# Inputs rearranged before launch, transposed activations, and a seven-slot weight ring in a float32 two-layer model kernel

## The chip, the cores and the metric

The kernel runs on one core of a Trainium2 chip. The metric is device time in microseconds (us), the median of several runs. The core has five engines with queues of their own: TensorE (PE in the rows, matrix products), VectorE (DVE), ScalarE (ACT), GpSimd (POOL) and SyncE (SP, which here only issues transfers), and sixteen DMA engines that move data between HBM and the on-chip memory. An engine works through its own queue in order and waits on semaphores for the others.

## The reference, cut to what matters

The program is a mixing layer followed by two attention-like layers, all in float32, on 256 tokens of width 2048. Only its start matters for the change:

```python
shift, scale, gate = split(silu(c) @ w_ada + b_ada, 3)            # w_ada is 2048 x 6144
shift_c, scale_c, _ = split(silu(c_ctx) @ w_ada + b_ada, 3)
hc = rmsnorm(ctx, g_pre) * (1 + scale_c) + shift_c                 # 256 context tokens
zc = hc @ w_in[:, :XBC_W + DT_W]
hx = rmsnorm(x, g_pre) * (1 + scale) + shift                       # 256 tokens
zx = hx @ w_in                                                     # w_in is 2048 x 12352
...
vn = rmsnorm(v, g_v)
sg = einsum('gqk,bckgd->bcqgd', w_s, vn) + b_s                     # 16 matrices of 128 x 128
...
x = x + gate * rmsnorm(mixed @ w_out, g_post)
```

Here rmsnorm divides a token's row by the root of its mean square. The products are made from float32 numbers split in a high and a low part (`w_hi`, `w_lo`, `h_hi`, `h_lo`), three passes for each product.

## The kernel before, in words

Every engine has its own block of code, and the order of its work is written out by hand; semaphores tie the engines together. Weights stream through four slots of 512 columns by 2 row blocks (`raw`), ScalarE makes the high part (`w_hi`), VectorE the low part (`w_lo`), and TensorE multiplies. A set of eight such units over the 2048 rows is a chunk.

The first part of the program, the prefix, does more at once. For both token sets `x` and `ctx` it needs the normalised rows transposed (`x_T`, features on the partitions), and for every feature the scale and shift from `w_ada` (`mod`). The prefix is a list, `PREFIX`, that TensorE walks through:

- `turn` (16 entries, L741): four 128x128 transposes of the normalised rows in `x_in` each; ScalarE and VectorE take turns in copying the results to `x_T`.
- `ada` (32 entries, eight groups e of four, L718): one 1 MB block of `w_ada` times the two vectors `silu(c)` and `silu(c_ctx)` in `c_wide`, four matrix products. The rows print two instructions for each of these products, so x8 is one block and x32 a whole group.
- `cols` (L726): after four blocks VectorE copies the sums out (`ada_rows`), TensorE transposes them, and VectorE makes two feature blocks of `mod` (L1943 to L1951). ScalarE then computes `h_f` and `h_hi` from `x_T` and `mod` (`modulate`, L1290) and VectorE the low part `h_lo` (`halve`, L2025).
- `w` (16 entries, L623): one unit of the first two chunks, 24 products for an even m, 16 for an odd m. Unit m needs `h` of the feature blocks of group m // 2.

From group 3 on the list repeats: four `ada`, unit 2e-3, `cols` e, unit 2e-2. After group 7 come units 13, 14 and 15, and then the chunk B1.

SyncE walks through `LOADS`: the same order, with each unit's load placed four entries ahead. A block of `w_ada` is two DMAs of 512 KB with rows of 1 KB (256 columns), and is put in one of six slots (three in `raw_early`, three in `raw_first`); from the seventh block on SyncE waits until TensorE has used the slot. `x` and `ctx` are loaded as rows (8 KB each) ahead of all this. GpSimd issues twelve small loads of vectors (bias, gains, convolution weights) as rows, which TensorE transposes (`turn_vec`, L706), and later, when TensorE has used 28 blocks, the rest of the constants.

Before the transposes, ScalarE squares the rows of `x_in` and sums them in the same instruction (L1270, four of 128x2048), VectorE makes means and reciprocals, and both scale the rows (L2018, L1279).

Later, in phase V, the sixteen matrices of `w_s` come as rows and are turned by TensorE in four hooks (`turn_ws`, L861) and copied by VectorE (`w_sT`, L2175). In phases S and O1 the gate third of `w_ada` comes in 32 blocks (`gate_w`).

Of the kernel before, what the change touches and what calls it, by code (L numbers as in the profile page):

```python
# [11 lines left out]
P = 128  # L12
# [45 lines left out]
VEC_ROWS = [sum(k for _, k in rows) for rows in VEC_TILES]  # L58
# [52 lines left out]
PREFIX = []  # L111
for _v in range(AW4):
    PREFIX += [("turn", 0, 4 * _v + x) for x in range(4)] + [("ada", 0, _v)]
# [85 lines left out]
def two_blocks_kernel(nc, ins, out):  # L199
# [34 lines left out]
    RAW6 = at("raw_first", 136, [P, 6, 4, 2, 256])  # L234
    RAW3 = at("raw_early", 48, [P, 3, 4, 2, 256])
    ada_raw = lambda n: (RAW3 if n < 3 else RAW6)[:, ada_slot(n)]
# [10 lines left out]
    IDR = at("ident_r", kb, [P, P], F32R); kb += 0.5  # L247
# [11 lines left out]
    XIN = at("x_in", 128, [P, 2, NT, D])  # L259
    XT = at("x_T", 80, [P, 2, KT, SEQ])  # L260
    JUNK = at("junk", 112, [P, D])
# [4 lines left out]
    VR = at("vec_rows", 184, [P, 4, P])  # L266
# [18 lines left out]
    WS = at("w_s_rows", 160, [P, MLP_G, P])  # L285
    WST = at("w_sT", 176, [P, MLP_G, P])
# [76 lines left out]
    with ctx:  # L363
        def sem(name):
# [10 lines left out]
        vec_turned, vec_ok, ada_done, ada_ok, mod_ok = sem("vec_turned"), sem("vec_ok"), sem("ada_done"), sem("ada_ok"), sem("mod_ok")  # L375
        xn_ok, rec_ok, xa_ok = sem("xn_ok"), sem("rec_ok"), sem("xa_ok")
        pair_ok, zero_ok = sem("ident_pair_ok"), sem("zero_ok")
        turned, h_ok = sem("turned"), sem("h_ok")
# [5 lines left out]
        ws_in, gv_in, ctx_in = sem("ws_in"), sem("gv_in"), sem("ctx_in")  # L384
        ws_turned, ws_ok, v_ok, vstd_ok, vn_ok, sg_done, sg_ok = (sem(n) for n in (
            "ws_turned", "ws_ok", "v_ok", "vstd_ok", "vn_ok", "sg_done", "sg_ok"))
# [37 lines left out]
        class Seq:  # L424
# [24 lines left out]
            "w_out_odd_2": dram["w_out_odd_2"][0], "w_ada": dram["w_ada"][0],  # L449
        }  # L450
        w_of = {n: w.rearrange("(t p) n -> p t n", p=P) for n, w in w_of.items()}

        def vec_load(eng, tiles, t0, names, signal):

            for t, rows in enumerate(tiles, t0):
                for n, k in rows:
                    if names is not None and (n in ("c", "c_ctx")) != (names == "c"):
                        continue
                    if n.startswith("conv_w"):
                        src = dram["conv_w"][0].rearrange("k (b p) -> (k b) p", p=P)  # L460
                        src = src[0:128] if n == "conv_w0" else src[128:160]
                    else:
                        a = dram[n]
                        while len(a.shape) > 1 and a.shape[0] == 1:
                            a = a[0]
                        src = a if len(a.shape) == 2 else a.rearrange("(r p) -> r p", p=P)
                    r0 = VEC[n][1]
                    eng.dma_start(VR[r0:r0 + k, t, :], src).then_inc(signal, 16)
# [133 lines left out]
        def _(pe):  # L602
# [126 lines left out]
            def turn(x):  # L729

                a, k0 = x // 8, x % 8 * 2
                if x == 0:
                    pe.wait_ge(xn_ok, 2)
# [2128 lines left out]
```

## Time and profile before

| what | value |
|---|---|
| median of 3 runs | 1957.72 us (1957.55 to 1961.33) |
| span of the profiled execution | 1955.8 us, first to last instruction |
| outside the span, median less span | 1.9 us |
| TensorE busy | 1909.1 us, 98% |
| VectorE, ScalarE, GpSimd busy | 62%, 51%, 5% |
| moved by DMA | 360.49 MB, mean 184 GB/s |
| mean granted TensorE clock | 0.993 |

The profiled execution has no time of its own beside its span, so the 1.9 us between the span and the median stand for what lies around it. Busy shares are of the span. A matrix product's printed duration runs past the start of the next, because they are pipelined: what counts in a stretch is the distance from one start to the next. The 40 slices of the page show a TensorE that is below 90% busy in the first slice only (each slice is 48.9 us), and DMA engines that are full in the first two and a half slices and half full later.

### The profile page before, as it was taken

What the parts mean: (1) busy time and instruction counts of PE and PEld (TensorE: products, weight loads), DVE (VectorE), ACT (ScalarE), POOL (GpSimd) and SP (SyncE); (2) the same over time, 40 slices, a digit from 0 to 9 for tenths busy, and PEclk for the clock granted to TensorE, in tenths of its full rate; (3) what the DMA queues carried; (4) which work ended last, traced back from release to release, by engine and by line L of the source; (5) the groups of instructions that cost most, each with busy time, mean ns of one, the idle gap of its engine ahead of it and who ended that gap; (6) DMA issues with size and microseconds to landing.
All of it is one profiled execution on the core that took longest, in us unless ns stands there. A gap on an engine that the chain in (4) does not pass through costs nothing.

```text
span 1955.8 us, 28973 instructions
## 1 busy us (share of the span) xinstructions
PE 1909.1 (98%) x11133; PEld 1608.1 (82%) x11133; DVE 1217.1 (62%) x1703; ACT 1000.0 (51%) x1464; POOL 106.6 (5%) x117
## 2 busy tenths in 40 slices
PE   5989999999999999999999999999999999999999
PEld 3558888898887777787888998878889999998887
DVE  3325655686558889867766687667555455555554
ACT  5435322345555666654446434667444555556642
POOL 1010000000023344000000000000000000000000
PEclk8989999999999999999999999999999999999999
DMA  9983322357657667758975555545566655555564
GB/s 341 349 255 108 100 85 86 87 171 226 191 175 196 183 174 202 234 175 264 357 249 153 151 152 162 171 142 152 181 186 176 181 171 162 173 164 170 167 188 163
DMA packets 210046, 360.49 MB, mean 184 GB/s; under 512 B 14264, under 2 KB 61776, under 8 KB 209024
## 3 DMA queue, kind: packets, MB, share of 16 engines
q1 hardware_dynamic: 200448, 349.36, 57.9%
q10 hardware_dynamic: 8848, 8.47, 2.1%
q8 instruction: 86, 1.41, 0.3%
q0 software_dynamic: 624, 0.92, 0.2%
q14 instruction: 40, 0.33, 0.1%
HBM read 356.55 MB, written 2.16 MB: 183 GB/s over the span
## 4 chain that ended last, share of the span: by engine, by line
PE 89%; DVE 3%; SPq 2%; DMA 1%; ACT 1%; issue 1%; DVEq 0%; ACTq 0%
PE acc L656 53%; PE acc L643 15%; PE acc L623 10%; DMA raw_first<-in_w_ada 1%; SPq L502 1%; PE side L902 1%; PE side L1029 1%; DVE conv L2088 1%; PE side L956 1%; PE side L891 1%; DVE w_lo L1921 1%; PE side L796 1%; PE side L623 0%; ACT w_hi L1241 0%; PE side L718 0%
## 5 line engine op out<-in xcount | busy, mean ns | idle before, releaser
L1921 DVE TENSOR_TENSOR w_lo<-raw,w_hi 128x1024 fp32r<-128x1024 f32 (+1 forms) x552 | 670.7, 1220 | 418.5 <-ACT w_hi L1241 412.5
L1241 ACT CAST w_hi<-raw 128x1024 fp32r<-128x1024 f32 (+1 forms) x544 | 561.0, 1035 | 607.9 <-PE acc L656 398.0
L656 PE MATMUL acc<-w_hi,h_hi 128*128 128x512 f32 (+1 forms) x1312 | 521.3, 397 | 2.5 <-DVE h_lo L2286 1.8
L656 PE MATMUL acc<-w_hi,h_lo 128*128 128x512 f32 (+1 forms) x1312 | 509.0, 388 | 0.0
L656 PE MATMUL acc<-w_lo,h_hi 128*128 128x512 f32 (+1 forms) x1312 | 508.3, 387 | 0.0
L656 PEld LDWEIGHTS acc<-w_hi,h_hi 128*128 128x128 f32 x1312 | 246.7, 188 | 52.8 <-DVE h_lo L2286 2.1
L656 PEld LDWEIGHTS acc<-w_hi,h_lo 128*128 128x128 f32 x1312 | 246.4, 188 | 51.1
L656 PEld LDWEIGHTS acc<-w_lo,h_hi 128*128 128x128 f32 x1312 | 246.9, 188 | 47.0
L643 PE MATMUL acc<-h_hi,w_hi 128*128 128x256 f32 x896 | 257.8, 288 | 1.0 <-DVE h_lo L2286 1.0
L643 PE MATMUL acc<-h_hi,w_lo 128*128 128x256 f32 x896 | 254.5, 284 | 0.0
L643 PE MATMUL acc<-h_lo,w_hi 128*128 128x256 f32 x896 | 254.5, 284 | 0.0
L643 PEld LDWEIGHTS acc<-h_hi,w_hi 128*128 128x128 f32 x896 | 172.9, 193 | 2.0 <-DVE h_lo L2286 1.4
L643 PEld LDWEIGHTS acc<-h_lo,w_hi 128*128 128x128 f32 x896 | 173.0, 193 | 0.2
L643 PEld LDWEIGHTS acc<-h_hi,w_lo 128*128 128x128 f32 x896 | 172.8, 193 | 0.0
L623 PE MATMUL acc<-h_hi,w_hi 128*128 128x512 f32 x352 | 141.4, 402 | 4.2 <-DVE w_lo L1921 3.0
L623 PE MATMUL acc<-h_hi,w_lo 128*128 128x512 f32 x352 | 138.4, 393 | 0.0
L623 PE MATMUL acc<-h_lo,w_hi 128*128 128x512 f32 x352 | 138.4, 393 | 0.0
L656 PE MATMUL acc<-w_hi,g_hi 128*128 128x512 f32 x256 | 101.0, 395 | 0.0
L656 PE MATMUL acc<-w_hi,g_lo 128*128 128x512 f32 x256 | 99.9, 390 | 0.0
L656 PE MATMUL acc<-w_lo,g_hi 128*128 128x512 f32 x256 | 99.7, 390 | 0.0
L623 PEld LDWEIGHTS acc<-h_hi,w_hi 128*128 128x128 f32 x352 | 66.8, 190 | 20.8 <-issue 3.8
L623 PEld LDWEIGHTS acc<-h_hi,w_lo 128*128 128x128 f32 x352 | 66.8, 190 | 14.5
(405 smaller groups left out, 1977.5 us busy)
## 6 DMA issues: line engine op xcount, KB each, us to landing
raw<-in_w_in SPq DMA_DIRECT2D x184, 512.0 KB, 4.2
raw<-in_w_in_odd SPq DMA_DIRECT2D x128, 512.0 KB, 3.7
raw<-in_w_in_even SPq DMA_DIRECT2D x96, 512.0 KB, 3.8
raw<-in_w_out SPq DMA_DIRECT2D x64, 512.0 KB, 5.0
raw_first<-in_w_ada SPq DMA_DIRECT2D x58, 512.0 KB, 8.8
gate_w<-in_w_ada SPq DMA_DIRECT2D x32, 512.0 KB, 6.4
raw<-in_w_out_even SPq DMA_DIRECT2D x32, 512.0 KB, 4.6
raw<-in_w_out_odd SPq DMA_DIRECT2D x32, 512.0 KB, 4.6
```

Of the source, the lines that this page charges most:

```text
L502: sp.dma_start(ada_raw(n)[:, :, h, :], w_of["w_ada"][:, 4 * u:4 * u + 4, h * D + e * 256:h * D + e * 256 + 256]).then_inc(ada_in[ada_slot( ...
L623: o = nc.tensor.matmul(bank[b][:].rearrange("p (a t) -> p a t", a=2), l, r, start=first and kk == 0 and x == 0, stop=last and kk == 1 and ...
L643: o = nc.tensor.matmul(ACC[b][:, (b4 % 2) * SEQ:(b4 % 2 + 1) * SEQ], l, r, start=first and kk == 0 and m == 0 and b4 % 2 == 0, stop=last a ...
L656: o = nc.tensor.matmul(ACC[b][:, 0:n], l, r, start=first and kk == 0 and m == 0, stop=last and kk == 1 and m == 2)
L796: o = nc.tensor.matmul(SB[d][:, g * 256:(g + 1) * 256], BG[:, t, g, :], XW[:, d, t, g * 256:(g + 1) * 256], start=t == 0, stop=t == NT - 1)
L891: o = nc.tensor.matmul(SB[3 - 2 * d][:, t * 256:(t + 1) * 256], GB[:, 1, t * P:(t + 1) * P], ST[:, d, bass.ds(g * 256, 256)], start=True, ...
L902: o = nc.tensor.matmul(SB[2][c:c + 64, t * 256 + r * HD:t * 256 + (r + 1) * HD], MM[:, r % 2, k, t * P + c:t * P + c + 64], XH[:, k, bass. ...
L956: o = nc.tensor.transpose(SB[b][:, k * SEQ + t * P:k * SEQ + (t + 1) * P], src[:, t, kt * P:(kt + 1) * P], con("ident"))
L1029: o = nc.tensor.matmul(later(SB[2 * (n % 2)][c:c + 64, o0:o0 + 64], l), KI[:, hb, h, k * P + c:k * P + c + 64], right(QD[:, hb, h, sl], l) ...
L1241: act.copy(WHI[:, u % 4, :, 0:n], RAW[:, u % 4, :, 0:n]).then_inc(hi_ready, 1)
L1921: dve.tensor_tensor(WLO[:, u % 4, :, 0:n], RAW[:, u % 4, :, 0:n], WHI[:, u % 4, :, 0:n].bitcast(F32), ALU.subtract).then_inc(lo_ready, 1)
L2088: seq(dve.scalar_tensor_tensor(v[:, 0:end], z[:, k:k + end], w(k), v[:, 0:end], ALU.mult, ALU.add))
```

## The change

The arrays are rearranged before the launch, outside the device time, and the kernel loads them in the form in which it uses them.

- `x` and `ctx` come transposed in four blocks of 1 MB (`x_cols`), straight into `x_T`. The 64 transposes, their copies and the scaling of rows go. The sums of squares are now over the transposed data: ScalarE squares 128x2048 blocks (`x_squares`), VectorE adds eight feature blocks per token (`x_reduce`, a reduction whose successive elements lie 1 KB apart), TensorE sums over the partitions with a vector of ones (`x_sums`) and spreads the reciprocal roots over all partitions (`x_rows`), ScalarE copies them (`x_rstd_rows`), and VectorE multiplies `x_T` by them, one feature block (128x512) at a time (`x_scale`): eight ahead of group 0, the other eight in pairs behind the groups 1 to 4.
- The small vectors come as columns in three DMAs; their transposes go.
- `w_ada` comes in contiguous blocks of 1 MB, 8 KB for each partition, one DMA each; the first weight units come in blocks with 4 KB or 2.5 KB for each partition. Ten blocks of `w_ada` fit before SyncE waits (three early slots used once, and a ring of seven).
- `w_s` comes transposed, so the sixteen transposes and four copies go. The gate blocks come contiguous, 4 KB for each partition.
- The low part of unit 0 is now made ahead of `halve` 0 and 1.

```diff
-PREFIX = []
-for _v in range(AW4):
-    PREFIX += [("turn", 0, 4 * _v + x) for x in range(4)] + [("ada", 0, _v)]
+PREFIX = [("ada", 0, v) for v in range(AW4)]
...
-    LOADS.insert(_at - (4 if _m < 14 else 0), ("w", 0, _m))
-VEC_AT = 14
+    LOADS.insert(max(AW4, _at - (4 if _m < 14 else 0)), ("w", 0, _m))
+EARLY, RING = 3, 7
...
-    return n if n < 6 else 3 + n % 3 if n % 6 < 3 else n % 3
+    return n if n < EARLY else EARLY + (n - EARLY) % RING
...
         def _(sp):
             sp.dma_start(CON[:, 0:P], dram["const_a"][:, 0:P]).then_inc(con_in, 16)
-            sp.dma_start(XIN[:, 0], dram["x"][0].rearrange("(t p) d -> p t d", p=P)).then_inc(x_in, 16)
-            sp.dma_start(XIN[:, 1], dram["ctx"][0].rearrange("(t p) d -> p t d", p=P)).then_inc(ctx_in, 16)
+            for i in range(4):
+                sp.dma_start(XT[:, i // 2, i % 2 * 8:i % 2 * 8 + 8, :].rearrange("p k t -> p (k t)"), dram["x_cols"][i]).then_inc(xt_in[i], 16)
             for kind, e, u in LOADS:
                 if kind == "ada":
                     n = AW4 * e + u
-                    if n == 9:
-                        sp.wait_ge(turned, KT)
-                    elif 6 <= n < 9:
-                        sp.wait_ge(ada_used, n - 2)
-                    elif n >= 12:
-                        sp.wait_ge(ada_used, n - 5)
-                    for h in range(2):
-                        sp.dma_start(ada_raw(n)[:, :, h, :],
-                                     w_of["w_ada"][:, 4 * u:4 * u + 4, h * D + e * 256:h * D + e * 256 + 256]
-                                     ).then_inc(ada_in[ada_slot(n)], 16)
+                    if n >= EARLY + RING:
+                        sp.wait_ge(ada_used, n - RING + 1)
+                    sp.dma_start(ada_raw(n).rearrange("p j h n -> p (j h n)"), dram["ada_units"][n]).then_inc(ada_in[ada_slot(n)], 16)
...
-            sp.dma_start(WS[:], dram["w_s"][0].rearrange("g q k -> q g k")).then_inc(ws_in, 16)
+            sp.dma_start(WST[:].rearrange("p g q -> p (g q)"), dram["w_s_cols"]).then_inc(ws_in, 16)
...
+            def x_sums():
+
+                pe.wait_ge(sc_ok, 3)
+                for a in range(2):
+                    pe.wait_ge(xss_ok, 2 * a + 2)
+                    for t in range(NT):
+                        for i in range(2):
+                            o = nc.tensor.matmul(ACC[0][:, 2 * a + t:2 * a + t + 1], SSX[:, 2 * a + i, t * P:(t + 1) * P],
+                                                 STAT[:, 63:64], start=i == 0, stop=i == 1)
+                o.then_inc(xsum_done, 1)
+
+            def x_rows():
+
+                pe.wait_ge(nrt_ok, 3)
+                for x in range(4):
+                    o = nc.tensor.matmul(ACC[1][:, x * P:(x + 1) * P], STAT[:, 12 + x:13 + x].to_broadcast([P, P]), con("ident"),
+                                         start=True, stop=True)
+                o.then_inc(xrow_done, 1)
...
+            def x_squares(i):
+
+                act.wait_ge(xt_in[i], 16)
+                if i >= 2:
+                    act.wait_ge(xss_ok, i - 1)
+                act.activation(SQX[i % 2][:], XT[:, i // 2, i % 2 * 8:i % 2 * 8 + 8, :], ACT.Square).then_inc(nsq_ok, 1)
...
+            def x_reduce(i):
+
+                dve.wait_ge(nsq_ok, i + 1)
+                dve.tensor_reduce(SSX[:, i, :], SQX[i % 2][:].rearrange("p k t -> p t k"), AX.X, ALU.add).then_inc(xss_ok, 1)
...
+            def x_scale(kt):
+
+                if kt == 0:
+                    dve.wait_ge(xrow_ok, 1)
+                dve.tensor_tensor(XT[:, :, kt, :], XT[:, :, kt, :], RBX[:], ALU.mult).then_inc(xr_ok, 1)
...
-            chunk("V", cV + 1, 1, hooks={u: (lambda u=u: turn_ws(u)) for u in range(4)})
+            chunk("V", cV + 1, 1)
```

TensorE at the start of the program, before:

```order
L699 MATMUL side<-con,vec_rows 128x32
L741 MATMUL acc<-con,x_in 128x128 x16
L718 MATMUL side<-raw_early,c_wide 32x512 x4
L741 MATMUL acc<-con,x_in 128x128 x16
L718 MATMUL side<-raw_early,c_wide 32x512 x4
L741 MATMUL acc<-con,x_in 128x128 x16
L718 MATMUL side<-raw_early,c_wide 32x512 x4
```

TensorE at the same place in the changed kernel (`x_square_sums` is what VectorE's reductions wrote, `stat` holds the vector of ones and the reciprocal roots):

```order
L691 MATMUL acc<-stat,x_square_sums 128x1 x8
L699 MATMUL acc<-con,stat 128x128 x4
L673 MATMUL side<-raw_early,c_wide 32x512 x12
L673 MATMUL side<-raw_first,c_wide 32x512 x4
L681 MATMUL side<-con,ada_rows 128x128 x4
L673 MATMUL side<-raw_first,c_wide 32x512 x8
```

The transposes between the first blocks are gone, and all four blocks of group 0 now stand behind twelve small products that need the sums of squares of all of `x` and `ctx`.

VectorE at the start, before:

```order
L1927 TENSOR_TENSOR ident_pair<-con 128x64
L2011 TENSOR_SCALAR stat<-stat 128x2
L2016 RECIPROCAL stat<-stat 128x2
L2018 TENSOR_SCALAR x_in<-x_in,stat 128x2048 x2
L1958 COPY x_T<-acc 128x512 x2
L2011 TENSOR_SCALAR stat<-stat 128x2
L2016 RECIPROCAL stat<-stat 128x2
L2018 TENSOR_SCALAR x_in<-x_in,stat 128x2048
L1958 COPY x_T<-acc 128x512 x6
L1934 COPY ada_rows<-side 128x512
```

VectorE at the start of the changed kernel:

```order
L1848 TENSOR_TENSOR ident_pair<-con 128x64
L1879 TENSOR_REDUCE x_square_sums<-x_squares_a 128x256
L1879 TENSOR_REDUCE x_square_sums<-x_squares_b 128x256
L1879 TENSOR_REDUCE x_square_sums<-x_squares_a 128x256
L1879 TENSOR_REDUCE x_square_sums<-x_squares_b 128x256
L1884 TENSOR_SCALAR stat<-acc 128x4
L1886 RECIPROCAL stat<-stat 128x4
L1892 TENSOR_TENSOR x_T<-x_T,x_rstd_rows 128x2x256 x8
L1855 COPY ada_rows<-side 128x512
```

Four reductions and eight products now stand ahead of the copy of the first group's sums, in place of three scalings and eight copies.

SyncE from its first transfer, before:

```order
L489 DMA con<-in_const_a 128x128
L490 DMA x_in<-in_x 128x2x2048
L491 DMA x_in<-in_ctx 128x2x2048
L502 DMA raw_early<-in_w_ada 128x4x256 x4
L513 DMA raw<-in_w_in 128x2x512
L502 DMA raw_early<-in_w_ada 128x4x256 x2
L502 DMA raw_first<-in_w_ada 128x4x256 x2
```

SyncE from its first transfer in the changed kernel:

```order
L468 DMA con<-in_const_a 128x128
L470 DMA x_T<-in_x_cols 128x2048 x4
L476 DMA raw_early<-in_ada_units 128x2048 x3
L476 DMA raw_first<-in_ada_units 128x2048
L481 DMA raw<-in_w_even 128x1024
L481 DMA raw<-in_w_odd 128x2x320
L476 DMA raw_first<-in_ada_units 128x2048 x4
```

A block of `w_ada` is one transfer now, and the first weight unit's load has moved behind the four blocks of group 0.

## Rows read from the trace of the kernel before

**Rows 1.** The page's head and TensorE's line: busy, share, instructions.

```profile
span 1955.8 us, 28973 instructions
PE 1909.1 (98%) x11133; PEld 1608.1 (82%) x11133; DVE 1217.1 (62%) x1703; ACT 1000.0 (51%) x1464; POOL 106.6 (5%) x117
```

**Rows 2.** TensorE's waits after 170 us, longest first.

```profile
PE side L956 <- DVE x L2357: 3.2, 1, 3.2
```

**Rows 3.** Stretches of the prefix: busy time, granted clock, DMA share, GB/s.

```profile
core 0: us, PE busy (x) PEld busy (x) DVE busy (x) ACT busy (x) POOL busy (x), PEclk, DMA share, GB/s
4.00:14.00 10.00, 0.31 (x1) 0.18 (x1) 0.39 (x2) 5.93 (x9) 3.47 (x8) 1.00 1.01 403
20.00:120.00 100.00, 89.71 (x512) 54.36 (x511) 34.92 (x93) 42.17 (x75) 2.15 (x4) 0.95 1.10 349
40.00:50.00 10.00, 9.51 (x36) 6.91 (x40) 1.15 (x3) 1.05 (x1) 0.00 (x0) 0.67 1.10 354
120.00:134.00 14.00, 9.40 (x45) 4.09 (x43) 0.97 (x5) 4.67 (x9) 0.00 (x0) 0.81 0.98 287
```

**Rows 4.** The chain that ended last, 100 to 170 us: start, length, what.

```profile
123.29 10.70 DMA raw_first<-in_w_ada
...
134.03 1.94 PE side L718 x8
...
141.17 0.44 PE side L726 x4
...
147.08 2.72 PE side L623 x12
...
159.81 5.44 PE acc L623 x24
```

**Rows 5.** TensorE's instructions in order of time: start, length, line, count, idle before.

```profile
20.63 1.94 PE L718 MATMUL side<-raw_early,c_wide 128*32 128x512 f32 x8
...
30.91 1.06 PE L718 MATMUL side<-raw_first,c_wide 128*32 128x512 f32 x8
...
40.49 0.77 PE L623 MATMUL acc<-h_hi,w_hi 128*128 128x512 f32 x1 [1.90 <-DVE w_lo L1921]
...
49.00 1.92 PE L718 MATMUL side<-raw_first,c_wide 128*32 128x512 f32 x16
...
68.25 3.64 PE L718 MATMUL side<-raw_first,c_wide 128*32 128x512 f32 x32 [0.96 <-DVE mod L1951]
...
81.62 2.78 PE L718 MATMUL side<-raw_first,c_wide 128*32 128x512 f32 x24
```

**Rows 6.** DMA packets of 20 to 120 us, then of 2 to 14 us.

```profile
DMA packets 34680, 34.94 MB, mean 349 GB/s; under 512 B 3006, under 2 KB 32860, under 8 KB 34673
...
DMA packets 1077, 4.42 MB, mean 369 GB/s; under 512 B 263, under 2 KB 552, under 8 KB 568
```

**Rows 7.** DMA issues of 0 to 170 us: size, median us to landing.

```profile
raw_first<-in_w_ada SPq DMA_DIRECT2D x58, 512.0 KB, 8.8
...
x_in<-in_ctx SPq DMA_DIRECT2D x1, 2048.0 KB, 13.4
```

**Rows 8.** ScalarE's square of one block; VectorE's reductions, mean ns of one.

```profile
17.18 1.91 ACT L1270 ACTIVATE junk<-x_in 128x2048 f32<-128x2048 f32 x1
...
L2541 DVE TENSOR_REDUCE soft<-p_a 128x1 f32<-128x128 f32 x16 | 4.6, 286 | 2.3
L2510 DVE TENSOR_REDUCE stat<-sq 128x16 f32<-128x1024 f32 x2 | 2.3, 1210 | 0.0
L1943 DVE TENSOR_REDUCE ada_parts<-side 128x8 f32<-128x32 f32 x8 | 1.5, 192 | 17.8 <-PE side L726 17.8
```

**Rows 9.** VectorE: the end of group 0's `mod`, and the second `halve`.

```profile
34.20 0.15 DVE L1951 SCALAR_TENSOR_TENSOR mod<-ada_v,vec_t 128x2 f32<-128x2 f32 x1
...
38.52 0.69 DVE L2025 TENSOR_TENSOR h_lo<-h_f,h_hi 128x512 fp32r<-128x512 f32 x1 [1.28 <-ACT h_hi L1290]
```

**Rows 10.** TensorE: one of the four hooks of `turn_ws`.

```profile
458.63 0.60 PE L861 MATMUL side<-con,w_s_rows 128*128 128x128 f32 x4
```

More of the change, by code:

```diff
@@ L57 @@
         _r += _k
-VEC_ROWS = [sum(k for _, k in rows) for rows in VEC_TILES]
 CONST = [("ident", 128), ("le", 128), ("lt", 128), ("ge", 128), ("gt", 128), ("one", 128),
@@ L448, in two_blocks_kernel @@
             "w_out_even_2": dram["w_out_even_2"][0], "w_in_odd_2": dram["w_in_odd_2"][0],
-            "w_out_odd_2": dram["w_out_odd_2"][0], "w_ada": dram["w_ada"][0],
+            "w_out_odd_2": dram["w_out_odd_2"][0],
         }
         w_of = {n: w.rearrange("(t p) n -> p t n", p=P) for n, w in w_of.items()}
[L453 to L468, printed above, removed]
         def split_steps(eng, one, ph, c, j, mid, evict, last=False, before_evict=3, start=3):
@@ L2025, in halve @@
                 dve.tensor_tensor(HLO[:, :, kt, :], f, HHI[:, :, kt, :].bitcast(F32), ALU.subtract).then_inc(h_ok, 1)
-            mean_in(0)
-            norm_in(0)
-            norm_in(1)
-            xt_out(1)
-            xt_out(3)
-            mean_in(1)
-            norm_in(2)
-            for x in range(5, KT, 2):
-                xt_out(x)
+            for i in range(4):
+                x_reduce(i)
+            x_mean()
+            for kt in range(8):
+                x_scale(kt)
             ada_out(0)
@@ L2054, in _ @@
             mod(1)
+            x_scale(8)
+            x_scale(9)
             first_lo(2)
@@ L2059, in _ @@
             mod(2)
+            x_scale(10)
+            x_scale(11)
             for e in range(3, UPC):
@@ L2066, in _ @@
                 mod(e)
+                if e < 5:
+                    x_scale(6 + 2 * e)
+                    x_scale(7 + 2 * e)
             first_lo(13)
@@ L2839, in _, with column_layouts, unit_layouts @@
             pool.tensor_scalar(NM3[:], con("ge"), -1e30, None, ALU.mult).then_inc(n3_ok, 1)
-_INS = ("x", "c", "ctx", "c_ctx", "w_ada", "b_ada", "g_pre", "g_post", "w_in", "conv_w", "conv_b", "dt_bias",
-        "a_log", "d_skip", "g_ssd", "g_v", "w_s", "b_s", "g_mlp", "w_out", "ln_even_2", "w_in_even_2",
-        "q_norm_a_2", "k_norm_a_2", "sinks_a_2", "lower_bounds_2", "g_norm_b_2", "w_out_even_2", "ln_odd_2",
-        "w_in_odd_2", "w_out_odd_2")
+_INS = ("x", "w_in", "dt_bias", "a_log", "d_skip", "g_v", "w_out", "w_in_even_2",
+        "q_norm_a_2", "k_norm_a_2", "sinks_a_2", "g_norm_b_2", "w_out_even_2", "w_in_odd_2", "w_out_odd_2")
+def column_layouts(inputs):
+    lay = np.ascontiguousarray
+    get = lambda n: np.asarray(inputs[n])
+    cols = lambda a: a.reshape(-1, P).T
+    conv = get("conv_w")[0].reshape(-1, P)
+    of = {n: get(n) for _t in VEC_TILES for n, _ in _t if not n.startswith("conv_w")}
+    of["conv_w0"], of["conv_w1"] = conv[0:128], conv[128:160]
+    vecs = np.zeros((P, 4, P), np.float32)
+    for n, (t, r, k) in VEC.items():
+        vecs[:, t, r:r + k] = cols(of[n])
+    x = np.stack([get("x")[0], get("ctx")[0]]).transpose(0, 2, 1).reshape(2, 2, 8, P, SEQ).transpose(0, 1, 3, 2, 4)
+    return {"vecs": vecs.reshape(P, 4 * P), "x_cols": lay(x).reshape(4, P, 8 * SEQ),
+            "w_s_cols": lay(get("w_s")[0].transpose(2, 0, 1)).reshape(P, MLP_G * P)}
+def unit_layouts(w_ada, w_in):
+    lay = np.ascontiguousarray
+    ada = w_ada[:, :2 * D].reshape(AW4, 4, P, 2, UPC, 256).transpose(4, 0, 2, 1, 3, 5)
+    gate = w_ada[:, 2 * D:].reshape(UPC, 2, P, 4, NCOL).transpose(3, 0, 2, 1, 4)
+    first = w_in.reshape(UPC, 2, P, IN_W).transpose(0, 2, 1, 3)
+    odd = np.concatenate([first[..., SSD_W + NCOL:SSD_W + NCOL + 256], first[..., XBC_W:XBC_W + DT_W]], -1)
+    return {"ada_units": lay(ada).reshape(UPC * AW4, P, 2048), "gate_units": lay(gate).reshape(32, P, 2 * NCOL),
+            "w_even": lay(first[..., SSD_W:SSD_W + NCOL]), "w_odd": lay(odd)}
 def kernel(**inputs):
```

196 lines of the change are left out of this document (60 added, 136 removed).

## The prediction

> **What bounds the kernel now.** I read the page's head first: TensorE is busy 1909 of 1955.8 us [rows 1], so only its idle and slow stretches, and work taken off it, can give anything. Then its waits: after the first 170 us the longest is 3.2 us [rows 2], so nearly everything that TensorE doesn't do at full pace lies in the prefix, and behind it TensorE is its own bound. In the prefix the stretches show another limit. From 20 to 120 us the DMA engines are full (share 1.10) and bring 349 GB/s, from 120 to 134 us 287 [rows 3]. The chain says the same: the last `ada` block lands at 134.0, and only then TensorE goes on [rows 4]. Its order of time shows what this costs. Group 3's first block starts at 68.25, group 4's at 81.62 [rows 5]: 13.37 us for four blocks, an odd unit, `cols` and an even unit, with no wait for a transfer. Groups 4 to 7 at that pace would end at 81.62 + 4 x 13.37 = 135.1; in fact unit 13, which follows them, starts at 147.08 [rows 4]. So 12.0 us of the prefix are waits for blocks and their after-effects (the clock had fallen: 0.81 granted in 120 to 134 us [rows 3]). The other part is the start: unit 0 begins only at 40.49 [rows 5].
>
> **Faster transfers.** The blocks go from rows of 1 KB to 8 KB. In 20 to 120 us nearly all packets were under 2 KB (32860 of 34680), at 349 GB/s. The rows of `x` and `ctx` are 8 KB: in 2 to 14 us about half of the 1077 packets, and nearly all bytes, are that large [rows 6], and 4 to 14 us ran at 403 GB/s [rows 3]. I take 403. What must land ahead of the last block: 4.2 MB of tokens, 32 blocks of 1.049 MB = 33.6, units 0 to 13 in 7 x (0.524 + 0.328) = 6.0, and about 1.0 of constants and vectors, 44.8 MB in all. 44.8 / 0.403 = 111 us, from 2.6 us on, with 2 us for the small packets and the landing: 116 us, 18 earlier than now. A group's 5.05 MB take 12.5 us, less than TensorE's 13.37, so in the middle of the prefix TensorE sets the pace. Seven slots cover the 9.7 us (13.37 less 3.64) in which TensorE runs units and uses no block: 3.7 blocks arrive in it. SyncE issues half as many DMAs; its issue was held by full queues, not on the path by itself, and I count nothing for it.
>
> The Trainium skill, HBM Reference, Specifications (TRN2), gives about 358 GB/s for each core with its pair busy, and more for a core alone. The trace's 403 is above that figure, which speaks against such a cap here. As an estimate from that page, at 358 the last block would land 14 us later than I forecast and the time would be about 1949; it is the rival on the rate below.
>
> **The new start.** `ctx` landed 13.4 us after its issue at 1.7, so at 15.1 [rows 7]; the same bytes in four blocks end then too. The last square takes 1.91 [rows 8]: 17.0. The reduction of 2048 elements is not in the trace. Two rows of the same operation, 286 ns for 128 elements and 1210 for 1024, give 1.03 ns an element and 2.3 us for 2048. Its elements lie 1 KB apart. The nearest strided row is L1943 (steps of 128 bytes, in the accumulator memory): 192 ns for 32 elements, where the line through the other two gives 187 [rows 8]. So I take no penalty: 19.3. Bounds: 2.2 us from below, and from above twice the pace, 4.4 us, since 32 elements are a poor witness for 2048. The Trainium skill, SBUF — State Buffer, in the part on the DMA port swizzle, says that successive accesses in one 16-byte line run at full rate and each crossing to a new line pays; by it all 2048 accesses pay. The strided row does not show that, but it is another memory.
>
> Behind the reduction: eight one-column products, mean, root, reciprocal, 1.3 us by the pace of such small steps; four products of the `cols` kind, at half clock, 0.7; so TensorE is free at 21.3. The copy takes 0.7, then eight `x_scale` at 0.6 (the `halve` form of 128x512, 0.69 printed, [rows 9]) end at 26.9. Meanwhile TensorE does group 0's blocks. At half clock a block is 1.94, at full clock 3.64 / 4 = 0.91 [rows 5]. The first two at half, two at full: 21.3 + 3.8 + 1.8 = 26.9, all landed by 25.6 (15.1 + 4 x 2.6). Before, group 0's last block ended at 31.97 [rows 5], `mod` at 34.35, and the second `halve` at 39.21 [rows 9]: 2.4 and 4.9 us. Then `mod` 0 is ready at 29.3 and unit 0 starts at 34.2, since its own low part no longer stands behind `halve`. That is 6.3 us earlier than 40.49.
>
> Unit 0 ran 40.49 to 49.00, 8.5 us, against 5.44 for the same 24 products at full clock [rows 4, 5]; the granted clock of 40 to 50 us was 0.67 [rows 3], after the sparse work of 32 to 40. The work ahead of unit 0 is just as sparse in the changed kernel, so I leave those 3 us in.
>
> **The sum.** Unit 0 starts at 34.2, ends at 42.7; from there to group 3 as before, 68.25 - 49.00 = 19.25, so 62.0; five groups of 13.37: 128.8; units 13 to 15, 159.81 - 147.08 = 12.7 [rows 4, 5]: 141.6. Before, B1 started at 159.81. Gain 18.2 = 6.3 of start + 12.0 of waits. The check of the cover: in this timetable the last group starts at 115.5 and wants its last block at 118.2; it lands at 116. So 2 us of slack, and each 2% of DMA rate is worth 2.2 us: this is the tightest joint of the forecast. The second eight `x_scale` (1.2 us in each of four groups) lie on VectorE, which is busy 35 of the 100 us from 20 to 120 [rows 3].
>
> Phase V loses four hooks of four transposes; like four of `cols`, 0.44 each time [rows 4, 10]: 1.8 us off a TensorE that waits for nothing there. The four copies on VectorE, and larger gate packets, are hidden behind TensorE and count nothing; the small vectors neither, as their transposes lay beside transfers.
>
> 18.2 + 1.8 = 20.0; 1955.8 - 20.0 = 1935.8 us of span. The median lies 1.9 above the span, so 1937.7. If unit 0 and the blocks run at full clock, TensorE would gain 3 more, but then the last block decides and only 2 come through: 1935.6. If all first blocks run at half clock, 1939.6. At 414 GB/s with everything warm, 1934. This case alone: 1933 to 1941.
>
> **Rivals.**
>
> *The rate stays (0.10).* 403 GB/s may come from early, lighter traffic and not from long rows. For it: only those 10 us show it, while 349 held over 100 us. Against it: the share of 1.10 with short rows and 1.01 with long ones [rows 3], so a full queue moved less per share. At 349, 44.8 MB take 128.4, so the last block lands at 2.6 + 128.4 + 2 = 133.0, hardly before today's 134.0; with 0.9 for its products, 13.4 - 3.6 = 9.7 for unit 11, `cols` and unit 12, and 12.7 for the rest, B1 starts at 156.3: a gain of 3.5 + 1.8, and 1952.4.
>
> *The strided reductions are at half pace (0.15).* Blocks land from 7.3 us on, the first square ends at 9.2, and four reductions of 4.4 follow without a gap: 26.8 in place of 19.3. All of group 0 moves by 7.5 us, TensorE bound from there, with full slots: 1945.2.
>
> *Slower than before (0.03).* The same place with a worse price. The gain of 20.0 is gone when four reductions end at 39.3, at 7.5 us each (3.6 ns an element); at 10 us each the start is 29.9 late and the time is 1947.6 + 20 = 1967.6. The strided row speaks against it: all its 192 ns over 32 elements are 6 ns each, but by the line through the other two rows 154 of them are fixed, which leaves 1.2.
>
> *No change (0.02).* The prefix is shorter, but the chunk behind it takes it back: TensorE waits there for VectorE's convolution and low parts, work that starts with the prefix's end and moves with it. I find nothing in it tied to absolute time, so this keeps a small chance; 1956.
>
> **How the numbers follow.** Forecast 0.70, the four rivals 0.30. 1933 to 1946 holds the forecast and the half-paced reductions, 0.83 less their own edges, about 0.8. The measurement of this kernel can tell some 0.2% (4 us) from no change. Faster: forecast, rate, half pace, 0.95, less a little for what I did not see: 0.94. Within 0.2%: 0.03. Slower: 0.03.
>
> **What would show it.** `x_square_sums` reductions of 2.3 us, the last ending near 19; `x_rstd_rows` at 22; unit 0 near 34; 395 to 410 GB/s while blocks stream; groups 13.4 us apart with no wait for `raw_first`; the first B1 unit near 142; no L861 rows. The forecast is wrong if the reductions print 4 us or more, if the rate is near 350, or if SyncE's slot waits leave the queues empty.

## The result, and the profile after

The changed kernel takes **1943.78 us** (median of 4, 1940.34 to 1947.53), the kernel before 1958.02 (median of 4, 1957.55 to 1961.33). The ratio is 0.9926 (95% interval 0.9911 to 0.9941), a gain of 14.2 us. The forecast was 1937.7, a gain of 20.0. So the sign was right, the time lies in the range of 1933 to 1946, and the gain was forecast 6 us too large. The range held because it had been drawn wide enough for reductions at half pace, which is near to what came.

The page of the changed kernel: its head, TensorE's line, its granted clock in the 40 slices, and two kinds of DMA issue. Compare [rows 1, 7].

```profile
span 1945.3 us, 28765 instructions
...
PE 1900.0 (98%) x11072; PEld 1604.8 (82%) x11072; DVE 1229.4 (63%) x1707; ACT 991.4 (51%) x1446; POOL 98.1 (5%) x107
...
PEclk8999999999999999999999999999999999999999
...
raw_first<-in_ada_units SPq DMA_DIRECT2D x29, 1024.0 KB, 10.3
```

The span is 10.5 us shorter, while the medians differ by 14.2. What lies outside the span is 2.2 us, where it was 1.9. The profiled execution was the slowest of the four. Their times, with the mean granted clock over the run, were 1947.53 (0.994), 1944.28 (0.996), 1943.29 (0.997) and 1940.34 (0.997). The kernel before spread over less than 4 us. Part of the explanation below is about those extra microseconds.

Stretches of the prefix, the same columns as [rows 3]:

```profile
4.00:14.00 10.00, 0.00 (x0) 0.00 (x0) 5.55 (x2) 6.56 (x5) 0.00 (x0) 1.00 1.02 423
...
20.00:120.00 100.00, 88.73 (x487) 55.49 (x488) 42.15 (x105) 38.58 (x70) 2.12 (x4) 0.95 0.97 378
40.00:50.00 10.00, 9.84 (x40) 6.90 (x40) 0.88 (x3) 0.90 (x1) 0.00 (x0) 0.69 1.01 411
60.00:70.00 10.00, 8.32 (x48) 5.61 (x52) 4.07 (x13) 3.61 (x7) 0.00 (x0) 1.00 1.02 421
120.00:134.00 14.00, 14.00 (x80) 9.20 (x79) 5.32 (x14) 6.36 (x12) 3.70 (x2) 1.00 0.29 84
```

While the queues are full, the core reads 411 to 423 GB/s, against 349 to 354 before. The mean of 20 to 120 us, 378, is lower, in part because the queues are idle at times: their share is 0.97. In 120 to 134 us TensorE is busy all the time at full clock, where it was busy 9.40 of 14 us at 0.81 before [rows 3]. The Trainium skill, HBM Reference, Specifications (TRN2), says that with both cores of a pair streaming each gets about 358 GB/s, and that one alone measures near 425. The trace agrees with the second figure: 423 in the first row.

The longest two waits of TensorE up to 160 us (total us, times, longest) are these; none of the others, 1.9 us at most, is for a transfer:

```profile
PE acc L691 <- DVE x_square_sums L1879: 20.9, 2, 15.8
PE side L673 <- DVE mod L1872: 2.9, 3, 1.0
```

Before, this one stood among them:

```profile
PE side L718 <- DMA raw_first<-in_w_ada: 8.1, 7, 2.6
```

The chain from group 3 to B1's first unit (start, length), which answers to [rows 4, 5]:

```profile
67.86 3.64 PE side L673 x32
...
121.33 3.57 PE side L673 x32
...
134.67 2.72 PE side L589 x12
...
147.40 5.44 PE acc L589 x24
```

Groups follow each other at 13.4 us with no gap: (121.33 - 67.86) / 4 = 13.37. B1 starts at 147.40 in place of 159.81, 12.4 earlier. The twelve microseconds of waits and their after-effects are all gained. The six of the earlier start are not, and VectorE's instructions in order of time show where they went:

```profile
8.45 3.65 DVE L1879 TENSOR_REDUCE x_square_sums<-x_squares_a 128x256 f32<-128x2048 f32 x1 [5.28 <-ACT x_squares_a L1200]
...
19.14 3.58 DVE L1879 TENSOR_REDUCE x_square_sums<-x_squares_b 128x256 f32<-128x2048 f32 x1
24.67 0.16 DVE L1884 TENSOR_SCALAR stat<-acc 128x4 f32<-128x4 f32 x1 [1.96 <-PE acc L691]
...
28.07 4.91 DVE L1892 TENSOR_TENSOR x_T<-x_T,x_rstd_rows 128x512 f32<-128x512 f32 x8 [2.79 <-ACT x_rstd_rows L1210]
32.90 0.68 DVE L1855 COPY ada_rows<-side 128x512 f32<-128x512 f32 x1
...
35.04 0.15 DVE L1872 SCALAR_TENSOR_TENSOR mod<-ada_v,vec_t 128x2 f32<-128x2 f32 x1
```

And TensorE's:

```profile
22.77 1.87 PE L691 MATMUL acc<-stat,x_square_sums 128*128 128x1 f32 x8 [5.14 <-DVE x_square_sums L1879]
25.34 2.08 PE L699 MATMUL acc<-con,stat 128*128 128x128 f32 x8 [0.70 <-DVE stat L1886]
27.35 3.65 PE L673 MATMUL side<-raw_early,c_wide 128*32 128x512 f32 x24
...
40.16 0.76 PE L589 MATMUL acc<-h_hi,w_hi 128*128 128x512 f32 x1 [1.93 <-issue]
...
48.64 1.92 PE L673 MATMUL side<-raw_first,c_wide 128*32 128x512 f32 x16
```

A reduction takes 3.65 us and not 2.3. The four of them stand end to end, so the last ends at 22.7. Then come the small products, with the short steps between them, until 27.4. Unit 0 starts at 40.16, 0.3 before the 40.49 of [rows 5]. The other traces say the same. With the old path of `x` unit 0 starts at 39.33 to 40.76 (before and the three runs named b_ below), with the new one and its strided reductions at 39.86 to 40.16 (this trace, a_same, a_ring4, a_rows). As built, the new path doesn't start unit 0 any earlier.

A word on the clock in this stretch. A block of `w_ada` (x8) takes 1.94 us in some rows and 1.03 to 1.07 in others, and the other small products vary in the same way. In this trace the profile's column of the granted clock prints 1.00 throughout the first 35 us, and shows the lower level (0.50) only later, at 36 to 46 us. So for the first 35 us "half pace" is read from durations alone; that it is the clock isn't shown. The prediction's "half clock" for this stretch is to be read in this way too.

### The profile page after: what moved, and what is told of

Read it like the earlier page. It is cut to its first block, busy times and chain, and to the rows that moved or that the text cites. A ratio compares the mean times of both kernels' runs of the same rounds, so it can differ in the third digit from the quotient of the medians.

```text
span 1945.3 us, 28765 instructions
## 1 busy us (share of the span) xinstructions
PE 1900.0 (98%) x11072; PEld 1604.8 (82%) x11072; DVE 1229.4 (63%) x1707; ACT 991.4 (51%) x1446; POOL 98.1 (5%) x107
## 4 chain that ended last, share of the span: by engine, by line
PE 87%; DVE 4%; issue 2%; ACT 2%; DMA 1%; POOL 0%; ACTq 0%; DVEq 0%; POOLq 0%
PE acc L622 50%; PE acc L609 15%; PE acc L589 12%; PE side L589 1%; DVE w_lo L1841 1%; PE side L673 1%; DMA raw<-in_w_in 1%; PE side L974 1%; DVE conv L2011 1%; PE side L901 1%; PE side L847 1%; ACT w_hi L1186 1%; PE side L748 1%; DMA ex_a<-acs_scratch 0%; PE side L1110 0%
## 5 line engine op out<-in xcount | busy, mean ns | idle before, releaser
L589 PEld LDWEIGHTS acc<-h_hi,w_hi 128*128 128x128 f32 x352 | 66.8, 190 | 21.0 <-issue 4.0
L589 PEld LDWEIGHTS acc<-h_hi,w_lo 128*128 128x128 f32 x352 | 66.8, 190 | 14.4
```

The source lines that it names most:

```text
L589: o = nc.tensor.matmul(bank[b][:].rearrange("p (a t) -> p a t", a=2), l, r, start=first and kk == 0 and x == 0, stop=last and kk == 1 and ...
```

## The experiments

Four theories stood against each other. The gain comes from the length of the DMA rows. It comes from the new path of `x`. It comes from the seventh slot. The start is late because of the stride of the reductions.

**b_blocks**: the kernel before, with only the blocks of `w_ada` laid out contiguously.

```diff
-                    for h in range(2):
-                        sp.dma_start(ada_raw(n)[:, :, h, :], w_of["w_ada"][...]).then_inc(ada_in[ada_slot(n)], 16)
+                    sp.dma_start(ada_raw(n).rearrange("p j h n -> p (j h n)"), dram["ada_units"][n]).then_inc(ada_in[ada_slot(n)], 16)
```

> The kernel before with one part of the change: the 32 blocks of w_ada come contiguous, 8 KB for each partition, one DMA each, into the same six slots; tokens, vectors, first weights and w_s as before. Theory (long rows give the rate, and the rate was the bound of groups 3 to 7): over 400 GB/s while blocks stream, no wait of TensorE for raw_first, groups 13.4 us apart, B1's first unit near 148, time 11 to 12.5 us below before. Rival (the deeper ring or the early ordering was needed too): waits for raw_first stay and the gain is under 6 us.

Measured: 1948.24 (1944.66 to 1949.57) against 1958.71, ratio 0.9948 (0.9935 to 0.9962). Stretches of b_blocks:

```profile
60.00:70.00 10.00, 9.04 (x59) 5.26 (x57) 1.60 (x9) 3.62 (x9) 0.00 (x0) 1.00 1.04 407
120.00:134.00 14.00, 14.00 (x81) 9.54 (x74) 6.57 (x16) 5.72 (x10) 3.70 (x2) 1.00 0.32 86
```

This one edit brings 10.5 us (interval 7.4 to 12.7) of the 14.2, with six slots and the old path of `x`; 11 to 12.5 were expected. Its B1 starts at 145.89, even before the changed kernel's 147.40, in an execution that was the fastest of its five. What the rest of the change adds to it, 3.7 us by the medians, isn't clear of the noise, since the intervals (7.4 to 12.7 and 11.6 to 17.4) overlap.

**a_rows**: the changed kernel with only the contiguous blocks undone (1 KB rows, two transfers a block, seven slots).

> The changed kernel with the blocks of w_ada loaded as before, in two DMAs each with rows of 1 KB, into the ring of seven. Theory: the rate falls to about 350 GB/s, TensorE waits for blocks again, B1's first unit at 155 to 159, time only 2 to 6 us below before (1.8 of it from w_s). Rival (the ring of seven, the transposed tokens or the other blocks pay): at least half of the changed kernel's gain stays, 7 us or more below before.

Measured: 1954.28 (1951.11 to 1955.61), ratio 0.9976 (0.9967 to 0.9985). One stretch, and TensorE's wait in the prefix:

```profile
60.00:70.00 10.00, 8.41 (x54) 4.95 (x56) 2.81 (x11) 3.78 (x8) 0.00 (x0) 1.00 1.09 357
```

```profile
PE side L676 <- DMA raw_first<-in_w_ada: 6.5, 7, 1.8
```

The rate is back at 357 GB/s, the waits are back, and B1 starts at 156.47, as expected. The time is 4.4 us below its own before, where the changed kernel is 14.2 below, so 9.8 us are lost. From both sides the layout of the blocks is worth about ten microseconds. With short rows the other parts still bring 2.9 to 6.5 us, but they aren't told apart.

The edit changes three things at once: the length of a row (1 KB to 8 KB), where the rows lie in HBM (spread over `w_ada`, or one behind another) and the number of transfers (two to one). SyncE's issues do stand on the chain before, but the queues were full there (share 1.10), so more issues alone would hardly have brought more. Length and place of the rows were not tried apart.

**a_contig**: the reduction runs over neighbouring elements, so that only the stride differs. Its sums are of other elements, and the right sums of squares are left out.

```diff
-                dve.tensor_reduce(SSX[:, i, :], SQX[i % 2][:].rearrange("p k t -> p t k"), AX.X, ALU.add)...
+                dve.tensor_reduce(SSX[:, i, :], SQX[i % 2][:].rearrange("p k t -> p (k t)").rearrange("p (t k) -> p t k", k=8), AX.X, ALU.add)...
```

> The changed kernel with each reduction of squares reading eight neighbouring elements instead of eight that lie 1 KB apart, so the sums are of other elements (the right sums of squares are left out); counts, outputs and order are unchanged. Theory (the stride makes a reduction 3.6 us instead of 2.3): reductions of 2.2 to 2.4 us, the last ends near 19, the time falls by 3 to 4 us against the changed kernel. Rival (256 short sums are slow whatever the stride): reductions stay at 3.6 us and the time does not move.

Measured: 1940.42 (1938.17 to 1940.78), ratio 0.991 (0.9895 to 0.9925). VectorE in order of time:

```profile
8.04 2.29 DVE L1879 TENSOR_REDUCE x_square_sums<-x_squares_a 128x256 f32<-128x2048 f32 x1 [4.90 <-ACT x_squares_a L1200]
...
16.28 2.29 DVE L1879 TENSOR_REDUCE x_square_sums<-x_squares_b 128x256 f32<-128x2048 f32 x1 [0.19 <-ACT x_squares_b L1200]
```

2.29 us is the 2.3 of the forecast, and the last reduction ends at 18.6. So the stride costs 1.36 us in each reduction, and 4.1 us at the end of the last; the time falls by about as much (18.3 us below before in place of 14.2). Unit 0 starts at 36.00 and B1 at 141.99. That this is near the 141.6 of the forecast is in part luck: unit 0 starts 1.8 us after the 34.2 forecast, and takes 7.2 us in place of 8.5.

**a_ring4**: four slots in place of seven (`EARLY, RING = 3, 4`).

> The changed kernel with a ring of four slots in place of seven. Theory (the rate pays, and TensorE's 9.7 us without blocks are covered by about four of them): time within 3 us of the changed kernel, few short waits for raw_first. Rival (the depth of the ring pays): TensorE waits some us in each of groups 3 to 7 and 6 us or more of the gain are lost.

Measured: 1948.99 (1948.1 to 1949.42), ratio 0.9952 (0.9938 to 0.9965), 9.7 us below before, so 4.5 less than the changed kernel. Its stretches and its chain:

```profile
40.00:60.00 20.00, 17.79 (x95) 10.81 (x96) 6.47 (x16) 6.23 (x11) 0.00 (x0) 0.91 0.67 256
60.00:80.00 20.00, 18.90 (x103) 12.93 (x101) 8.64 (x26) 9.91 (x19) 0.00 (x0) 1.00 1.01 416
```

```profile
58.20 11.17 DMA raw_first<-in_ada_units
110.58 15.08 DMA raw_first<-in_ada_units
```

While TensorE runs units and takes no block, four slots fill up and the queues stand idle (share 0.67). Two blocks then lie on the chain. The result is between the two expectations. The intervals of the two ratios touch, but all five executions are slower than all four of the changed kernel, and the trace shows the idle queues: four slots are too few. With six, b_blocks shows no wait for a block.

**a_same**: the changed kernel once more, in the second batch, as a measure of its spread.

> The changed kernel once more, unchanged, beside its variants on one chip. Every theory: 1940 to 1947 us, 12 to 17 us below before, with a spread of some us between executions from stretches at half clock.

Measured: 1943.13 (1942.05 to 1947.42) against 1957.06, ratio 0.9932 (0.9918 to 0.9945). One stretch of its trace:

```profile
40.00:50.00 10.00, 10.00 (x51) 6.85 (x52) 1.33 (x3) 0.66 (x1) 0.00 (x0) 1.00 1.02 414
```

Unit 0 starts at 39.92, but here it ran at full clock (1.00, where the other execution had 0.69) and took 5.65 us in place of 8.5. So B1 starts at 144.33, 3.1 us before that of the other execution of the same kernel.

**a_tree**: each reduction becomes three additions of whole tiles (8 rows of 256 to 4, 2, 1).

```diff
-                dve.tensor_reduce(SSX[:, i, :], SQX[i % 2][:].rearrange("p k t -> p t k"), AX.X, ALU.add)...
+                q = SQX[i % 2]
+                seq(dve.tensor_tensor(q[:, 0:4, :], q[:, 0:4, :], q[:, 4:8, :], ALU.add))
+                seq(dve.tensor_tensor(q[:, 0:2, :], q[:, 0:2, :], q[:, 2:4, :], ALU.add))
+                dve.tensor_tensor(SSX[:, i, :], q[:, 0, :], q[:, 1, :], ALU.add)...
```

> The changed kernel with each strided reduction of squares replaced by three additions of neighbouring halves (128x1024, 128x512, 128x256), with the right sums. Theory (the stride alone was the price, 1.2 us a block over contiguous work): 2.4 to 2.6 us a block, last sum near 19, unit 0 near 36.5, time 3 to 4 us below the changed kernel. Rival (the saved time is swallowed by the wait for group 0's fourth block of w_ada): unit 0 stays near 40, time within 1 us of the changed kernel.

Measured: 1941.87 (1940.68 to 1943.32), ratio 0.9919 (0.9906 to 0.9933). VectorE in order of time:

```profile
7.98 1.23 DVE L1880 TENSOR_TENSOR x_squares_a<-x_squares_a 128x1024 f32<-128x1024 f32 x1 [4.86 <-ACT x_squares_a L1200]
9.24 0.69 DVE L1881 TENSOR_TENSOR x_squares_a<-x_squares_a 128x512 f32<-128x512 f32 x1
9.96 0.42 DVE L1882 TENSOR_TENSOR x_square_sums<-x_squares_a 128x256 f32<-128x256 f32 x1
```

A block's sums take 2.4 us, the last ends at 18.7 and unit 0 starts at 36.08, all as expected. But the granted clock was 0.50 for 5.9 of unit 0's 8.46 us, and the median is only 1.3 below that of a_same, where 3 to 4 were expected.

**f_order** moves the small products behind group 0's third block (the sums) and fourth block (the rows), and spreads the scalings among unit 0's steps. **f_tree** is f_order and a_tree together.

> The changed kernel, with the strided reductions as they are, but group 0's blocks of w_ada ahead of the sums on TensorE, and only two of the eight early scalings ahead of group 0's scale and shift on VectorE, the others in its gaps. Theory (the start is a chain of sums, spreading, eight scalings and then group 0, and TensorE has nothing else to do in it): group 0's mod near 29 instead of 35, unit 0 near 34 instead of 40, time 5 to 6.5 us below the changed kernel. Rival (after such a start the transfers bind again): unit 0 near 34, but waits for raw_first in later groups give it back, under 2.5 us.

> Both edits, the new order and the three additions. Theory: with the new order group 0's own blocks (the fourth lands near 25) and the first scalings are nearly level, so the additions give only 0 to 1.5 us more than the order alone. Rival (the sums are still the last to arrive): another 3 to 4 us.

Measured: f_order 1941.33 (1938.63 to 1943.62), ratio 0.9921 (0.9907 to 0.9934); f_tree 1941.09 (1939.05 to 1943.05), ratio 0.9916 (0.9902 to 0.9929). TensorE in order of time, first f_order, then f_tree:

```profile
23.67 3.58 PE L691 MATMUL acc<-stat,x_square_sums 128*128 128x1 f32 x16
...
29.03 2.08 PE L699 MATMUL acc<-con,stat 128*128 128x128 f32 x8
...
38.80 0.53 PE L589 MATMUL acc<-h_hi,w_hi 128*128 128x512 f32 x1 [2.98 <-issue]
```

```profile
23.40 1.95 PE L691 MATMUL acc<-stat,x_square_sums 128*128 128x1 f32 x16
...
26.27 1.16 PE L699 MATMUL acc<-con,stat 128*128 128x128 f32 x8
...
35.11 0.47 PE L589 MATMUL acc<-h_hi,w_hi 128*128 128x512 f32 x1 [2.46 <-issue]
```

The order brings less than expected: unit 0 at 38.80 and not 34, and a median 1.8 us below a_same and not 5 to 6.5. In f_order the products run at half pace, where eight products of one column cost 3.58 us. In f_tree the same ones take 1.95, at full pace. Unit 0 starts 3.7 us earlier there, and B1 at 141.12 against 144.78. Yet the medians are 0.2 apart.

**f_split** is f_tree with the sums in two halves, one behind each of the first two blocks, and the rows behind the third. **f_warm** is f_split with products that compute nothing in TensorE's idle time (nine before the first block, four and five later).

```diff
+            pe.wait_ge(xt_in[0], 16)
+            filler(9, XT[:, 0, 0:2, :].rearrange("p k t -> p (k t)"))
...
+                if (kind, r, u) == ("ada", 1, 0):
+                    pe.wait_ge(xrow_ok, 1)
+                    filler(4, old)
+                if (kind, r, u) == ("w", 0, 0):
+                    filler(5, old)
```

> As f_tree, but TensorE takes the sums of each half as soon as it is there: block, sums of x, block, sums of ctx, block, spreading, block. In f_tree the sums stood behind three blocks at half clock. Theory: group 0's mod near 29 instead of 30.1, unit 0 near 34, time 1 us below f_tree, about 1940. Rival (group 0's fourth block and its scale and shift decide, whatever the place of the sums): unit 0 stays near 35, no change.

> As f_split, with filler products on TensorE whose results nobody reads: 9 while it waits for the tokens, 4 after group 0's cols, 5 ahead of unit 0. Theory (the half-clock stretch at 36 to 46 us comes after sparse work, and costs 1.5 to 3 us in unit 0 by itself): no half-clock stretch from 17 to 60 us, unit 0 lasts 5.5 us instead of 7 to 8.5, time 2 to 3 us below f_split. Rival (the fillers are in the way, or the clock falls anyway): the same or slower.

Measured: f_split 1942.61 (1940.01 to 1945.37), ratio 0.9918 (0.9905 to 0.9932); f_warm 1943.69 (1939.61 to 1943.98), ratio 0.9919 (0.9905 to 0.9932). Stretches of f_split, then of f_warm:

```profile
40.00:60.00 20.00, 17.83 (x96) 10.76 (x95) 6.50 (x16) 5.61 (x10) 0.00 (x0) 0.91 1.02 414
```

```profile
40.00:60.00 20.00, 17.83 (x104) 10.94 (x103) 5.72 (x14) 5.61 (x10) 0.00 (x0) 1.00 1.02 415
212.00:222.00 10.00, 9.48 (x48) 8.20 (x47) 7.78 (x9) 4.12 (x11) 1.53 (x1) 0.70 0.54 169
```

Both miss what was expected of them. f_split's unit 0 starts at 37.66 and not 34, 2.5 us after that of f_tree, and no gain is left. With the fillers unit 0 takes 5.98 us (8.5 in f_split) and B1 starts at 143.28 (144.88). But the granted clock still fell at 22 to 28 us, unit 0 also ran at full clock in a_same, which has no fillers, and one trace of each doesn't show that they were the cause. Later in this trace the clock falls at 216 us, 0.70 over ten microseconds, and the time is no shorter.

**b_ws**: the kernel before, with only `w_s` transposed. **b_blocks_ws**: this and b_blocks together.

```diff
-            sp.dma_start(WS[:], dram["w_s"][0].rearrange("g q k -> q g k")).then_inc(ws_in, 16)
+            sp.dma_start(WST[:].rearrange("p g q -> p (g q)"), dram["w_s_cols"]).then_inc(ws_in, 16)
...
-            chunk("V", cV + 1, 1, hooks={u: (lambda u=u: turn_ws(u)) for u in range(4)})
+            chunk("V", cV + 1, 1)
```

> The kernel before with only w_s transposed before the launch. Theory: sixteen transposes of 0.11 us off a full TensorE, 1.8 us faster, 1955 to 1956. Rival (hidden, or given back at the loop's end): no change.

> The kernel before with contiguous blocks of w_ada and w_s transposed, and nothing else: tokens as rows with TensorE's transposes, six slots, first weights and vectors as before. Theory (these two parts are the whole gain, and the transposed tokens bring nothing): 12 to 13.5 us below before, level with the changed kernel within 2 us; unit 0 near 39.3. Rival (the transposed tokens, the seventh slot or the other blocks bring part of it): 3 us or more slower than the changed kernel's distance of 14.

Measured: b_ws 1957.26 (1955.81 to 1959.52) against 1957.49, ratio 0.9998 (0.9989 to 1.0007); b_blocks_ws 1945.8 (1941.46 to 1949.23), ratio 0.9938 (0.9924 to 0.9951). The interval of b_ws, a gain of -1.4 to +2.2 us, holds both nothing and the 1.8 expected. Two stretches of b_ws, then the same two of the kernel before:

```profile
230.00:240.00 10.00, 10.00 (x55) 8.62 (x55) 6.96 (x8) 3.59 (x8) 1.20 (x1) 0.83 0.54 164
890.00:900.00 10.00, 8.16 (x31) 6.35 (x30) 5.69 (x9) 3.82 (x6) 0.00 (x0) 0.83 0.84 263
```

```profile
230.00:240.00 10.00, 9.72 (x60) 8.58 (x61) 7.58 (x9) 4.05 (x9) 1.54 (x1) 1.00 0.54 164
890.00:900.00 10.00, 8.16 (x38) 6.50 (x38) 7.12 (x11) 5.36 (x8) 0.00 (x0) 1.00 0.83 272
```

At two places b_ws granted 0.83 over ten microseconds where the kernel before had 1.00. b_blocks_ws is 11.7 us below before, against 10.5 for b_blocks in its batch. The intervals overlap, so what `w_s` adds there can't be told from nothing either. 11.7 is just under the 12 to 13.5 of its theory and 2.5 less than the changed kernel's 14.2, where the rival wanted 3 or more: whether the transposed tokens bring anything stays open.

## Why the prediction was right, and where it was too large

**Faster transfers: right.** 403 GB/s was forecast, 411 to 423 came. The wait for `raw_first`, 8.1 us before, went to zero, and the groups run at 13.37 us. The 12.0 us read out of [rows 3 to 5] are what came: the gain at B1 is 12.4, of which 0.3 is start. b_blocks and a_rows tie this to the layout of the blocks, by 10.5 and 9.8 us from the two sides; that the length of the rows is what counts in it is likely but not shown by itself. What the seventh slot adds to six wasn't tried by itself; no wait is left for it to remove.

**The new start: mis-sized.** The step that failed is the chain to unit 0, forecast for 34.2 and found at 40.16. Two terms carry it.

- The reductions. "So I take no penalty: 19.3" became 22.7, which is 3.4 us later. a_contig shows that the stride is the cause. L1943's strided row [rows 8] was a poor witness, in another memory and of few elements, as the prediction said itself. The time of 3.65 lies within the bounds of 2.2 and 4.4, and this rival had its place in the range. The Trainium skill, SBUF — State Buffer, in the part on the DMA port swizzle, says that an access pays when it crosses to a new 16-byte line. The runs agree in direction: 3.65 us against 2.29.
- The small products. From the last reduction to the end of the rows 2.0 us were forecast (1.3 and 0.7), and 4.7 came: 1.87 for four products of one column, some 0.7 for mean, root and reciprocal, 2.08 for four of the rows. f_order has both kinds at half pace: four of the rows take 2.08 us and print as x8, four transposes of `cols` take 1.06 and print as x4. So the witness for the rows was of the wrong kind, with one instruction where the rows have two. At full pace, as in f_tree, the rows would still have taken 1.16.

Together 3.4 + 2.7 = 6.1 us, and the rest of the chain was as forecast: `x_scale` 4.91 (4.9), `mod` 2.3 us later (2.4), unit 0 after another 5.0 (4.9).

**What follows unit 0: right.** It took 8.5 us at the clock of 0.69, as assumed, which is luck in part, since in a_same it took 5.65. Then 19.2 to group 3 (19.25), 66.8 for five groups (66.85), 12.73 to B1 (12.7).

**`w_s`: seen in the trace, not in the time.** From phase V's first product to the state products, the kernel before takes 576.30 - 234.53 = 341.8 us and the changed one 563.49 - 223.62 = 339.9. That is the 1.8 of the forecast. The other traces agree: the same stretch takes 341.8 in b_blocks, the other kernel with the old `w_s`, and 339.8 to 339.9 in seven of the twelve with the new one (up to 342.2 in the rest). But b_ws by itself is worth 0.2 us by medians, with an interval of about -1.4 to +2.2, which neither shows the 1.8 nor rules it out. Its trace loses clock at two places, but one profile isn't the 11 runs. So the products are gone and the stretch is shorter; that the total is, stays open.

**The clock behind the prefix: not foreseen.** The forecast carried the gain of the prefix to the end unchanged, and in the profiled execution it wasn't. The difference between before and after is 12.4 at B1, 10.9 at the first long product of phase V, 12.8 at 576 us, 12.8 at 879, 11.0 at 1061, 10.9 at VectorE's last instruction, and 10.5 at the end. The two large losses are half-clock stretches; the last 0.4 us lie behind the last computation, where only the store of the result is left, and aren't explained. This is the first, as TensorE's order of time in the changed kernel and before:

```profile
220.87 2.82 PE L770 MATMUL side<-con,dt_a 128*64 128x128 f32 x12
```

```profile
233.08 1.52 PE L818 MATMUL side<-con,dt_a 128*64 128x128 f32 x12
```

The second is at 883 us. Stretches of the changed kernel at both places:

```profile
220.00:224.00 4.00, 4.00 (x21) 3.56 (x21) 3.89 (x6) 0.27 (x2) 0.00 (x0) 0.57 0.82 223
...
882.00:886.00 4.00, 4.00 (x13) 3.09 (x12) 2.27 (x4) 0.00 (x0) 0.00 (x0) 0.57 0.62 201
```

The same twelve products take 2.82 us for 1.52, with nothing changed in them. These stretches come and go. a_same has only the second, a_contig neither, b_ws both. Where the rows can be counted, they cost about 1.5 and 1.8 us. A third, at 1010 to 1050 us, is in all fourteen traces, and about as long before (0.82 and 0.83 over ten microseconds each) as after (0.79 and 0.87), so it takes nothing from the difference. With the start as measured, 12.4 + 1.9 - 0.4 = 13.9 would be the gain without the first two, and the medians say 14.2. That fits with typical executions of the changed kernel that lose no more clock than those of before, as their mean clocks of 0.996 and 0.997 suggest. It isn't shown, since each measurement has a trace of one execution only. No run settles what makes the clock fall there in one execution and not in the next.

**The rivals.** The rate stayed up. The reductions cost 1.6 times the forecast, so "half pace" was nearer than the main line in mechanism, and its 1945.2 is also nearer to 1943.8 than the 1937.7 of the main line. "Slower" would have needed 7.5 us a reduction. "No change" failed: the prefix's gain is 12.4 at B1 and, but for the clock, holds to the end.

**Is there a better version?** a_contig (1940.4, with other sums), f_tree (1941.1), f_order (1941.3) and a_tree (1941.9) all lie 15 to 18 us below before, and the changed kernel 14. f_tree has the earliest B1 of them, 6.3 us before the profiled changed kernel. But its interval of 0.9902 to 0.9929 overlaps the 0.9918 to 0.9945 of a_same. f_split (14.9 below) and f_warm (13.8) are no better. So none of them is shown to beat the changed kernel.

## What to carry to other kernels

Where the DMA share is at 1.1 and the packets are small, lay the operand out so that each partition reads one long row out of a contiguous block, and look at the rate of a stretch that already has long rows for what it will bring. Size a new operation by a row of its own kind, stride and memory; where there is none, run the edit with the stride taken out, which costs one run and settles it. Where the work ahead of a stage is sparse, price small products at half pace, count the instructions that the rows print for each, and don't read a gain of one or two microseconds out of a single trace, since the clock can fall or stay up in the next.

## What the runs showed of the hardware

- Loads of contiguous blocks with 8 KB rows ran at 407 to 423 GB/s with a share of 1.01 to 1.04, those with 1 KB rows at 349 to 357 with a share of 1.09 to 1.10. A busy queue alone doesn't say that the bytes come at their best rate.
- Summing 128x2048 fp32 elements eight at a time took 3.65 us with neighbours 1 KB apart and 2.29 us side by side. Three additions of whole rows, 1.23 + 0.69 + 0.42, give the same sums in 2.4 us.
- Eight fp32 products of one column took 3.58 us in f_order and 1.95 in f_tree, 0.45 and 0.24 us each, while the profile printed a granted clock of 1.00 in both.
- In a kernel whose TensorE is 98% busy, the granted clock falls to the 1.2 GHz level for some microseconds at 216 to 233 and at 877 to 896 us in some executions. Small products and short waits lie at the first place (2.48 of 3.00 us busy in 217 to 220), but before has them too, without the fall. Unit 0, at 36 to 49 us, ran between 5.65 and 8.5 us in traces of the same kernel.
